# Setup taken by quarters of the features, and the attention's output gate by halves of the tokens over jobs 0 to 29

## What is computed

```python
mod_x = silu(c) @ w_mod + b_mod            # 1024 -> 3 * 1024: shift, scale, gate
hx = rmsnorm(x, norm_g) * (1 + sc_x) + sh_x      # 512 tokens; hc likewise, 256 tokens
z = hx @ w_in                              # aq, ak, av, ag, alr, ... by columns
alog = log_sigmoid(alr @ gla_up + gla_ub) / 16   # decay of the GLA mixer
oa, state = gla_chunked(aq, ak, av, alog, state) # chunks of 64 tokens, two directions
...
# each of the two layers of the second block
a_q, ..., z = split(rms_norm(x) @ w_in_2)        # z: 1024 columns
mixed = concat([o_a, o_b, o_c]) * silu(z)        # the output gate
x = x + rms_norm(mixed @ w_out, g_post)
```

## Time and profile before

| | us |
|---|---|
| median of 3 runs | 1315.31 |
| the profiled execution's span, first to last instruction | 1313.0 |
| what lies around the span (median less span) | 2.3 |
| TensorE busy in the span | 1266.9 |
| VectorE, ScalarE, GpSimd busy | 698.7, 417.0, 398.1 |

### The profile page before, as it was taken

One profiled execution on the slowest core, in us unless ns is written; L12 is line 12 of the kernel. 1 busy time (PEld: TensorE's weight loads), 2 busy tenths in 40 slices (PEclk: granted clock), 3 DMA queues, 4 the chain that ended last, 5 costly groups with the idle time before them and its releaser, 6 DMA issues.

```text
span 1313.0 us, 24617 instructions
## 1 busy us (share of the span) xinstructions
PE 1266.9 (96%) x9971; PEld 772.5 (59%) x9971; DVE 698.7 (53%) x1422; ACT 417.0 (32%) x904; POOL 398.1 (30%) x470
## 2 busy tenths in 40 slices
PE   5999999999999999999999999999999999999997
PEld 3454655555656666687445885446645786455553
DVE  4356567847234444573473563247646373237745
ACT  4243213253433332101024002347613102236721
POOL 0100000202334443181432320225761250115671
PEclk9999999999999999999999999999999999999999
DMA  9710112011130100042426315110004415100001
GB/s 308 288 64 0 67 66 80 26 39 65 66 130 3 67 3 3 2 153 104 147 74 137 97 32 192 65 53 1 2 16 98 135 33 192 65 1 2 1 1 64
DMA packets 71535, 96.59 MB, mean 74 GB/s; under 512 B 27639, under 2 KB 35247, under 8 KB 71422
## 3 DMA queue, kind: packets, MB, share of 16 engines
q1 hardware_dynamic: 71050, 94.76, 21.7%
q10 hardware_dynamic: 372, 0.27, 0.1%
HBM read 92.89 MB, written 2.13 MB: 72 GB/s over the span
## 4 chain that ended last, share of the span: by engine, by line
PE 85%; DVE 6%; SPq 3%; ACT 3%; issue 1%; DMA 1%; POOL 0%; DVEq 0%; POOLq 0%; ACTq 0%
PE PS L147 81%; PE PS L2830 2%; DVE AR L2936 2%; ACT AR L3058 1%; SPq L187 1%; DMA bias_rows<-AR 1%; DVE AR L2923 1%; SPq L304 1%; SPq L308 1%; ACT AR L3068 0%; SPq L309 0%; SPq L312 0%; DVE AR L2106 0%; DVE AR L866 0%; PE PS L2164 0%
## 5 line engine op out<-in xcount | busy, mean ns | idle before, releaser
L147 PE MATMUL PS<-AR 64*64 64x64 f32 (+13 forms) x9334 | 1196.2, 326 | 21.8 <-ACT AR L3068 6.0
L147 PEld LDWEIGHTS PS<-AR 64*64 64x64 f32 (+5 forms) x9334 | 703.0, 152 | 485.1 <-issue 384.7
L3058 ACT ACTIVATE AR<-AR 128x257 f32<-128x257 f32 (+5 forms) x160 | 84.9, 531 | 96.1 <-DVE AR L2936 86.1
L2936 DVE CUSTOM_DVE_ANT_0 AR<-PS,AR 128x257 f32<-128x257 f32 (+5 forms) x160 | 72.2, 451 | 60.5 <-PE PS L147 43.0
L412 POOL TENSOR_TENSOR AR<-AR 128x1 f32<-128x1 f32 (+4 forms) x26 | 21.9, 841 | 258.6 <-DVE AR L407 211.8
L1189 DVE SCALAR_TENSOR_TENSOR AR<-AR 128x441 f32<-128x441 f32 (+2 forms) x96 | 78.6, 819 | 15.7 <-ACT AR L1146 12.0
L3119 POOL TENSOR_SCALAR AR<-AR 128x257 f32<-128x257 f32 (+5 forms) x96 | 53.4, 556 | 75.8 <-DVE AR L2942 70.3
L1612 DVE TENSOR_TENSOR AR<-PS,AR 128x256 f32<-128x256 f32 x60 | 25.5, 424 | 85.7 <-PE PS L147 82.4
L3117 POOL TENSOR_SCALAR AR<-AR 128x128 f32<-128x128 f32 (+3 forms) x64 | 39.0, 609 | 68.4 <-DVE AR L2942 64.5
L2053 POOL TENSOR_TENSOR AR<-AR 128x512 f32<-128x512 f32 x36 | 49.6, 1377 | 29.0 <-DMA AR<-in_w_o 26.0
L1738 ACT ACTIVATE AR<-PS 128x512 f32<-128x512 f32 x48 | 28.7, 597 | 82.5 <-PE PS L147 80.3
(11 more groups left out here) (264 smaller groups left out, 964.8 us busy)
## 6 DMA issues: line engine op xcount, KB each, us to landing
AR<-in_w_in SPq DMA_DIRECT2D x16, 2048.0 KB, 9.1
AR<-in_w_mod SPq DMA_DIRECT2D x6, 2048.0 KB, 13.1
AR<-in_w_out SPq DMA_DIRECT2D x4, 2048.0 KB, 13.0
AR<-in_x SPq DMA_DIRECT2D x8, 512.0 KB, 5.1
AR<-in_w_in SPq DMA_DIRECT2D x4, 1024.0 KB, 7.4
AR<-in_w_o SPq DMA_DIRECT2D x2, 2048.0 KB, 8.2
AR<-in_w_in SPq DMA_DIRECT2D x2, 1664.0 KB, 8.7
AR<-in_w_in SPq DMA_DIRECT2D x12, 256.0 KB, 4.2
```

Of the source, the lines that this page charges most:

```text
L147: return t.matmul(o, l, r, start=s, stop=p, skip_group_check=True)
L2936: v.do.tensor_tensor_reduce(PB[j % NJP][e][:, 0:nk], ps["s", l, j, e][:, 0:nk], bias_for(qb, kind, 2 * a + e, nk), 1.0, 3e38, ALU.add, ALU ...
L3058: a_.do.activation(P, P, ACT.Exp, bias=mn[:, j % NJS, e:e + 1], scale=-1.0, accum_out=su[:, j % NJS, e:e + 1]).then_inc(sa, na("p", l, j, e))
```

## The change

*Setup by quarters.* `mod(k)` now takes shift and scale of one quarter of the features (256 columns of each, two DMAs of 1 MB), so one `turned(k)` gives both for two tiles of features. TensorE turns x row by row as each row is scaled, four transposes to a bank, first thing; the small transposes and the bias rows (`brow`) come after. `low_rank`, `queries` and, newly, `keys` go by quarters: three quarters of the queries and keys stand ahead of `u`, the last quarter behind `bb`. The context rows are loaded, squared and turned later. The two context keys share a bank and are copied by one VectorE instruction. `gla_ends_t(t, 0, i)` stands after value tile 4, no longer after 2. `gla_up` is loaded and its memset done in setup.

*Gate by halves.* The six gate tiles are done first for tokens 0 to 255 (4 matmuls of 256 columns per job, jobs 0 to 11, banks 2 and 5 in turn), then for tokens 256 to 511 (3, 3 and 2 matmuls per job, jobs 12 to 29, all in bank 2). Scores of jobs 13 to 30 use banks 5, 0, 1 and transposes only 3, 4.

```diff
-        for half, ks in ((0, (0, 2)), (1, (1, 3))):
-            for k in ks:
-                s.go.dma_start(wmod[:, k], wm(512 * k)[0]).then_inc(s_wm[k], 16)
+        for k in range(4):
+            for j in range(2):
+                s.go.dma_start(wmod[:, k, :, 256 * j:256 * j + 256], wm(1024 * j + 256 * k, 256)[0]).then_inc(s_wm[k], 16)
...
+            s.go.dma_start(aq[:, sl, :], wl[1][0][0][:, sl, :]).then_inc(s_aq[k] if k < 3 else s_ring[ring_slot(1)], 16)
+            if k == 0:
+                for i in range(2):
+                    s.go.dma_start(xsv[:, i, :], I["ctx"][0, 128 * i:128 * i + 128, :]).then_inc(s_x[i], 16)
...
+    def turned_tokens(t, name, row, banks):
+        t.wait_ge(sv, nv["xn", row])
+        for i in range(2):
+            p = ps.take(t, name, row, i, bank=banks[i])
+            for m in range(4):
+                x = t.go.transpose(p[:, 128 * m:128 * m + 128], xsv[:, row, 512 * i + 128 * m:512 * i + 128 * m + 128], ident)
...
     def setup_t(t):
         t.wait_ge(s_cst, 16)
+        for a in range(4):
+            turned_tokens(t, "hT", 2 + a, (2 * a, 2 * a + 1))
...
+        mod_turned(0)
+        low_rank(t, 0, 256)
+        queries(t, 0, 0)
+        queries(t, 1, 0)
+        for a in range(2):
+            turned_tokens(t, "hC", a, (1, 0))
+        keys(t, 0, 256, 0)
+        mod(1)
...
     def gla_t(t):
-        low_rank(t, 1)
-        queries(t, 0, 4, 8)
+        keys(t, 0, 0, 2)
+        keys(t, 1, 0, 2)
+        keys(t, 1, 256, 2)
+        ps.ring = [0, 4, 5]
         t.wait_ge(s_up, 64)
         t.wait_ge(sv, nv["alr", 0])
...
-        queries(t, 1, 4, 8)
-        key(0)
-        key(1)
+        for a in range(2):
+            queries(t, a, 3)
+        keys(t, 0, 256, 3)
+        for a in range(2):
+            keys(t, a, 0, 3)
+        keys(t, 1, 256, 3)
...
-            if a == 2:
+            if a == 4:
                 for i in range(4):
                     gla_ends_t(t, 0, i)
...
         keys_of(0)
+        keys_of_context()
         gla_sums_v(v, 0)
+        keys_of(1)
         gla_sums_v(v, 1)
-        keys_of(1)
...
-    GATES = [(m, i) for m in (5, 4, 1, 0, 3, 2) for i in range(8)]
-    PER_JOB = 4
-    FILLED = len(GATES) // PER_JOB
+    GATE_TILES = (5, 4, 1, 0, 3, 2)
+    GATES = [(m, half, i) for half in range(2) for m in GATE_TILES for i in range(8)]
+    FIRST_JOBS, FILLED = 12, 30
...
+        j, k = divmod(max(0, i - FIRST_JOBS), 3)
+        x = GATES[4 * i:4 * i + 4] if i < FIRST_JOBS else GATES[48 + 8 * j + 3 * k:48 + 8 * j + min(8, 3 * k + 3)]
+            ps.take(t, "sz", l, m, half, bank=2 if half else (2, 5)[m % 2])
...
-        few = itertools.cycle((0, 1)), itertools.cycle((3, 4))
-        all_ = itertools.cycle((2, 0, 1)), itertools.cycle((5, 3, 4))
+        rings_of = ((itertools.cycle((0, 1)), itertools.cycle((3, 4))), (itertools.cycle((5, 0, 1)), itertools.cycle((3, 4))),
+                    (itertools.cycle((5, 0, 1)), itertools.cycle((2, 3, 4))))
```

More of the change, by code:

```diff
@@ L342, in mod_turned @@
             t.wait_ge(sv, nv["mrow", k])
[L343 removed]
+            p = ps.take(t, "modT", k, bank=0)
             for m in range(4):
[L345 removed]
+                x = mm(t.go, p[:, 2 * m:2 * m + 2], mrow[:, 512 * (k % 2) + 128 * m:512 * (k % 2) + 128 * m + 128], sel, True, True)
             x.then_inc(st, nt("modT", k))
[L348 to L349 removed]
@@ L350, in setup_t @@
[L350 to L354, removed]
         t.wait_ge(sa, na["silu_c"])
-        ps.ring = list(range(8))
         mod(0)
[L358 to L363, removed]
+        t.wait_ge(s_oh, 32)
@@ L371, in setup_t @@
+        low_rank(t, 2, 256)
+        low_rank(t, 2, 0)
         mod(3)
-        queries(t, 1, 0, 2)
+        queries(t, 0, 2)
+        queries(t, 1, 2)
         mod_turned(3)
-        queries(t, 1, 2, 4)
+        keys(t, 0, 256, 2)
+        low_rank(t, 3, 256)
+        low_rank(t, 3, 0)
         nt.mark("at", "setup")
-    def low_rank(t, half):
-        w, = weights(t, 0)
[L381 to L392, removed]
-            nt.mark("weights", 0)
@@ L395, in queries, with features @@
[L395 to L402, removed]
-            x.then_inc(st, nt("aq", a))
+    def features(t, lo, k):
+        hx, h = (hT, "hT") if lo else (hC, "hC")
+        for t8 in (2 * k, 2 * k + 1):
+            t.wait_ge(*((sa, na[h, t8]) if t8 % 2 else (sv, nv[h, t8])))
+        return hx
@@ new lines, in low_rank, with query_key_weights @@
+    def low_rank(t, k, lo):
+        w, = weights(t, 0)
+        hx, n = features(t, lo, k), 512 if lo else 256
+        b = 4 if lo else 5
+        p = ps.banks[b] if k else ps.take(t, "alr", lo, bank=b)
+        for q in range(2):
+            x = mm(t.go, p[64 * q:64 * q + 64, 0:n], w[:, 2 * k + q, :], hx[:, 2 * k + q, :], k == 0, k == 3)
+        if k == 3:
+            x.then_inc(st, nt("alr", lo))
+            nt.mark("weights", 0)
+    def query_key_weights(t, k):
+        if k < 3:
+            t.wait_ge(s_aq[k], 16)
+            return wviews(1)[0]
+        return weights(t, 1)[0]
@@ new lines, in queries, with keys @@
+    def queries(t, a, k):
+        w = query_key_weights(t, k)
+        hx = features(t, 256, k)
+        p = ps.banks[6 + a] if k else ps.take(t, "aq", a, bank=6 + a)
+        for t8 in (2 * k, 2 * k + 1):
+            x = mm(t.go, p[:, :], w[:, t8, 128 * a:128 * a + 128], hx[:, t8, :], t8 == 0, t8 == 7)
+        if k == 3:
+            x.then_inc(st, nt("aq", a))
+    def keys(t, a, lo, k):
+        w = query_key_weights(t, k)
+        hx = features(t, lo, k)
+        b = 2 + a if lo else 1
+        p = ps.banks[b] if k or not lo and a else ps.take(t, "ak", a, lo, bank=b)
+        p = p if lo else p[:, 256 * a:256 * a + 256]
+        for t8 in (2 * k, 2 * k + 1):
+            x = mm(t.go, p, w[:, t8, 256 + 128 * a:384 + 128 * a], hx[:, t8, :], t8 == 0 and (lo > 0 or a == 0), t8 == 7)
+        if k == 3:
+            x.then_inc(st, nt("ak", a, lo))
@@ L477, in setup_v @@
-        turned(1)
-        row(3)
-        turned(3)
-        modulated(1)
+        for a in range(2):
+            normed(a)
+        for a in range(2):
+            turned_tokens_v("hC", hC, a, a)
+        modulated(0, hC, "hC", 8)
+        for k in range(1, 4):
+            row(k)
+            turned(k)
+            modulated(k, hT, "hT", 0)
+            modulated(k, hC, "hC", 8)
         nv.mark("at", "setup")
@@ L2887, in filled @@
         def filled(i):
-            for m, k in gates_in(i)[0]:
-                out_gate(t, l, m, k, bank=(2, 5)[m % 2])
+            for m, half, k in gates_in(i)[0]:
+                half_gate(t, l, m, half, k)
         for i in range(NJ + PV):
-            rings = few if i <= FILLED else all_
+            rings = rings_of[(i > FIRST_JOBS) + (i > FILLED)]
             if i % 2 == 0:
```

236 lines of the change are left out of this document (127 added, 109 removed).

## The result

The changed kernel takes **1340.1 us** (median of 4 runs, 1339.77 to 1340.44) against 1315.24 of the kernel before on the same chip: a ratio of 1.0191, 95% interval 1.0178 to 1.0205. It is slower by 24.9 us. The forecast was 1331.3 with a range to 1338: the direction holds, the size does not. The profiled execution has a span of 1338.6, 25.6 over the 1313.0 of before.

What follows compares the result with a forecast made beforehand. The prediction took TensorE, busy 1266.9 of 1313.0 us, to bound the kernel. 1313.0 + 12.4 (wait at the sums) + 2.0 (low clock) + 1.6 (gate) = 1329.0, plus 2.3 around it: 1331.3 us, range 1318 to 1338.

Steps and rivals of the forecast that it cites:

- The wait ahead of the sums: GLA stage: TensorE idle some 12.5 us until ScalarE's value copy, so the stage ends 12.4 us later.
- The chain behind them: GLA stage, ends' transposes to sums: ScalarE and VectorE keep their order, so 122.7 leads to 143.4 us.
- Low clock after the wait: Behind the idle time at the sums: clock at its low level, +2.0 us, bounds 1.7 and 3.4.
- The waits of even steps for bank 2: Attention steps 12, 18, 24: new gate tile waits for the last one's read, 1.2 then about 1.5 us, 4.1 together.
- The front, "+0.6": Setup up to `u`: reordered transposes, bias rows and context sum to +0.6 us, bounds -3.5 and +3; `u` at 72.9.
- "+0.8 a layer": Attention, gate by halves: added waits 6.2 against 5.0 won, partly overlapping, +0.8 us a layer, +1.6 in all.
- "All that follows on every engine is shifted with it": After the GLA stage: everything moves by the stage's 12.4 us delay, since meeting points let no engine run ahead.
- "Behind `u` the covers have shrunk, the chain has not": From `u` to the sums: 15.5 us of keys moved ahead of `u`, while the chain keeps its length.
- That filling pays more than the setup costs: Rival: attention waits of 8.5 us a layer go and setup sees no low clock, 1309 us; 7%.
- that attention gains: Rival: attention wins 5 us a layer, the sums wait anyway, 1319.7 us; 13%.
- that nothing changes: Rival: no difference, within 0.2% of the kernel before; 4%.
- Transposes do not raise the clock: Rival, setup's front: opening transposes, first modulation and bias rows run low until about 27 us, 3 us more, 1334; 7%.

Runs made afterwards that it cites:

- the gate alone: The change's gate by halves on the setup of the kernel before; 1317.9 us, ratio 1.0029.
- the pause: The gate alone, but from job 12 on the first of each three jobs has no gate matmul and the others four each; 1310.2 us, ratio 0.9962.
- the rotation by itself: The kernel before with only the PSUM bank rotation set to the third bank behind the GLA stage; 1316.8 us, ratio 1.0018.
- the keys behind `u`: The setup alone with all keys behind `u` and `bb` again and the ends' transposes behind value tile 2; 1329.8 us.
- the setup alone: The change's setup by quarters on the attention of the kernel before; 1334.2 us, ratio 1.0142.
- the modulation ahead: The keys behind `u`, plus each quarter's modulation row one quarter earlier, turned rows in their own bank, context steps moved back; 1324.0 us.
- the pause at the end of three jobs: The gate alone with four, four and no gate matmuls in each three jobs from job 12; 1327.7 us.
- The row-wise start with the pause: The kernel before with x turned row by row first, plus the gate by halves with the pause; 1311.0 us, ratio 0.9975.
- the half tiles at the old places: The kernel before with each gate tile of jobs 0 to 11 split into two of 256 columns, one a job, banks 2 and 5; 1313.3 us, ratio 0.9990.

## Why the prediction was right or wrong

**Right.** The wait ahead of the sums: forecast idle for some 12.5 us, measured 12.39, ended by ScalarE's value copy. The ends' transposes at once when reached, forecast 122.7, measured 124.08. The chain behind them, forecast 20.7 from the transposes to the sums (122.7 to 143.4), measured 20.7. Low clock after the wait, forecast 2.0, measured 2.3 (88 records in 4.89 us at 0.50). The waits of even steps for bank 2: forecast 1.2 to 1.5 each, measured up to 1.8. Half tiles cost nothing.

**Wrong, by term.** The forecast adds 12.4 + 2.0 + 1.6 = 16.0 us to the span, measured are 25.6, so 9.6 are missing:

- *The front, "+0.6": 1.4 of the 9.6.* `u` was forecast at 72.9; VectorE reads it at 75.34, and the read stands 1.17 behind the start before, so `u` starts near 74.2. "Bounds -3.5 (no low clock at all) and +3" took the low stretch as one that could only shorten; it is 6.83 us long instead of 3.41, and TensorE works for 5.52 us of it instead of 3.41, which makes about 1.1 more at half speed. This carries through to the sums (+13.8 for "+12.4"). The low clock behind the wait adds 0.3 (2.3 for "+2.0").
- *"+0.8 a layer" for the gate: 5.0.* The measured loss is 3.2 and 3.4. The net of waits gained and lost was sized nearly right: the gate alone, in a profile without low clock in the attention, loses (38.51 + 63.89 - 1.73) - 99.35 = 1.3 us in layer 0 and 1.7 in layer 1. What was missing is that a wait of 1.83 us can bring a stretch of 3.41 us at 0.50: 1.7 a layer, 3.4 in all. I had charged a low clock to the 12 us wait only, though the earlier trace rows showed one right behind the wait of 1.14 that ends at 32.91. The gain was put too high besides: with the gate waits gone (the pause) jobs 0 to 29 gain 99.35 - (98.78 - 1.73) = 2.3 us in layer 0 and 2.0 in layer 1, where the forecast less its gate waits comes to 5.0 - 1.3 = 3.7. That the net came out near is in part luck.
- *No term at all for the PSUM rotation: 2.4.* "All that follows on every engine is shifted with it" was false: +1.9 ahead of layer 1 and some 0.5 at the end, close to the 2.2 of the rotation by itself. The order of the instructions does not show this, the bank numbers do.

The remaining 0.45 lie in the rest of the first block. Of the 9.6, some 4.5 are low clock (1.1 and 3.4), in the front and in the attention, that follows on waits under 2 us. So the steps that failed are these three: the low clock was charged to the long wait alone, the low stretch of the front was not allowed to grow, and the bank rotation had no term.

**Right in sum, incomplete in reason.** "Behind `u` the covers have shrunk, the chain has not" located the 12 us wait, but the keys are the smaller part of the cost: 4.4 of the 19.4 us. From VectorE's first read of `u` to the first sum it is 73.0 us before, 73.4 with the keys behind `u`, and 69.5 in the setup alone and in the changed kernel. So 15.5 us of keys ahead of `u` shorten what follows by 3.9 only, the wait takes up the rest, and they make `u` 5.2 later; the low clock behind the wait comes on top. The larger part lies in the quarters: a chain of small steps four times over holds `u` back to 70 even with no key ahead of it, where halves reach it at 56.8. Taking the modulation ahead gave 6.5 of these 13.3 us back; which of its moves did so was not taken apart, and the rest stays unexplained. The expectation of that run shows that I had not seen it.

**The rivals.** That filling pays more than the setup costs, that attention gains and that nothing changes are out. *Transposes do not raise the clock* is out as well. TensorE did transposes alone from 15.12 on, and in the windows above it goes from 9 records in 1.50 us to 11 in 1.00, at 20.0 us, which is where the trace's clock record opens; over all transposes of that line (shortest, median, longest ns), and below it those of the attention in the stretch of 880.16 to 883.57, whose granted clock is on record as 0.50:

```profile
L328 PE MATMUL PS<-AR x48: 272/287/447, 15.1 to 37.6; 128*128 128x128 f32 x48
```

```profile
L2904 PE MATMUL PS<-AR x3: 364/421/421, 883.0 to 883.4; 128*128 128x128 f32 x3
```

The first 32 start at 421 ns, the length at the low level (1.2 GHz), and end at 273, the length at the full one (2.4 GHz), with nothing else on TensorE. The Trainium skill ("TensorE: Matmul & The Clock Gate", Part 4: PE-mode transpose) has it that transposes do not count as activity for the clock; this trace, of float32 transposes, speaks against it.

**What stays open.** The +0.45 in the rest of the first block; why the pause at the end of three jobs costs 17 us more than at their beginning; what holds `u` at 64.8 with the modulation ahead, against 58.0; and which of two equal waits brings a low stretch.

## What to carry to other kernels

Where one kind of tile has a single bank, look for new tiles that wait for the full read of the last one, as here (4.4 us in layer 0). Before looking for another bank, leave a step without that tile: one changed slice turned a loss of 3.1 us into a gain of 4.6. Try more than one place for it, since the pause two jobs later lost 12.7. When work is cut into finer pieces, count the chain of small steps once per piece, and ask when the stage's critical value starts, not only what covers it. And compare the bank numbers of untouched code too, since a shared rotation carries a change into places hundreds of microseconds away.

## What the hardware showed that I had not expected

Low clock stretches within these profiles are 3.41, 6.83 or 13.65 us long, and a wait of 1.6 to 1.8 us brings one in some places and not in others. The profile with the keys behind `u` shows both: from 40 us on four waits of 1.59 or 1.60 us end at 45.59, 57.69, 67.07 and 70.18, and only behind the first of them the granted clock is 0.50 (45.63 to 49.04). Such a wait can therefore cost nearly twice its length, 1.83 us and 1.7 in the attention of the changed kernel.

It probably scatters the time as well. The nine runs of the gate alone differ by up to 4.4 us, with mean clocks of 0.998 and 0.994. The row-wise start with the pause has five runs at 1309.7 to 1310.2, three at 1314.2 to 1314.5 and two between. The mean clock does not settle it: it also counts stretches in which TensorE has no work, and the half tiles at the old places take 1313.1 to 1313.4 at 0.994 and 0.995, where the other runs of that kernel take 1313.2 to 1313.7 at 0.996 and 0.997.
